# In the head slots of an attention kernel, turn the next pair's weights ahead of the last pair's attend

## The chip, the cores and the metric

One core of a Trainium2 chip. The metric is device time of one execution in microseconds (us), as the median of several runs. TensorE multiplies, VectorE (DVE), ScalarE (ACT) and GpSimd (POOL) work beside it, and SyncE (SP) issues the loads of the weights.

## What is computed

Two blocks in float32 on 256 tokens with 2048 channels. The first has two layers, each of a projection into seven parts, a gated depthwise convolution with LayerNorm, and a windowed attention with 16 heads of 64 and a sink logit; then an output projection, an embedding term and a gate. The second has one "fox" layer (32 heads, causal, with forget gates) and one sliding-window layer (32 heads, rotary positions, sink). The attention is where the change lies; in the first block it is

```python
s = jnp.einsum('bqkgd,bskd->bkgqs', qb, kb) * scale + bias_band
m = jnp.maximum(jnp.max(s, axis=-1), sink_f)
e = jnp.exp(s - m[..., None])
denom = jnp.sum(e, axis=-1) + jnp.exp(sink_f - m)
pr = (e / denom[..., None]).astype(vb.dtype)
return jnp.einsum('bkgqs,bskd->bqkgd', pr, vb)
```

and the causal ones do the same with a causal or a sliding mask. With 256 tokens there are two blocks of 128 queries and two of 128 keys.

## The kernel before

**Gemms.** Every projection is a chunk of 512 output columns and 2048 input channels. It is cut into 8 pieces of 256 channels. A piece is loaded by SP into one of four places of a ring (`stage`, L280 to L288), split by ScalarE into a rounded part `w_hi` (L1534) and by VectorE into the rest `w_lo` (L913), and used by TensorE with three terms (`w_hi` x high, `w_lo` x high, `w_hi` x low, L495 and L506). In the form "T" (weights stationary, L495) a piece is 24 products of 256 columns: two steps of 12. In the form "N" (L506) it is 12 products of 512 columns.

**Slots.** After each of the 16 steps of a chunk stands a slot, in which TensorE does other work (L512 to L515). The dictionary `work` says which: the functions in the list of slot n are called in their order, and so stand in TensorE's queue, which runs in order. Each of the other engines has a list of its own, written by hand as hooks behind its pieces (`chunk` at L915 and L1536).

**Attention.** Heads come in groups of 8, four pairs per group. One chunk of TensorE holds a group's scores (L596, into PSUM banks). VectorE adds the bias and finds the maxima (L1007), ScalarE takes the exponentials (L1543) into the tile `u`, VectorE divides by the sums in two lots of four heads (`norms`, L1024 to L1040, event `normed`). The next chunk has the group's `heads` (L651) in its slots, two steps apart from one another:

- `turn(kind, i)` (L612 to L624) transposes pair i's weights from `u` into the banks TB and SB, one head each: per head 4 transposes of 128x128 if all blocks count ("full", first block), 3 if causal. It waits for `t_free` (all copies so far are done, so the banks are free) and `normed`, and counts `pt_done` for each head.
- ScalarE copies each head's turned weights from its bank to the tile `pt` (`copy_turned`, L1593 to L1600), waits for `pt_done` and counts `t_free`.
- `attend(kind, i, values)` (L626 to L649) multiplies the values with pair i's turned weights in `pt` into the banks OB and MB, the two heads into the two halves of the output partitions. It waits for `t_free`, for i = 0 also for `s_free` and `ob_free`.

There is one `pt` for all pairs, so pair i+1 may be copied only once pair i has been attended. The group's five slots are: turn 0; attend 0, turn 1; attend 1, turn 2; attend 2, turn 3; attend 3. When `att_done` has come for all heads, VectorE multiplies by the gate (`gated`, L1042).

There are 12 such groups: 2 per layer of the first block (L765, L767, "full"), 4 in the fox layer (L825, in a loop of 3 and once more) and 4 in the sliding-window layer (L884, a loop of 3; the last, L887 to L889, in chunks of form "N"). `again(name, back)` (L97) gives a wait for the count that the event has reached so far in the engine's own order, less `back`.

`pt` also takes the 256 channels of `p` at the start of each layer of the first block (L1650), behind all attends.

Of the kernel before, what the change touches and what calls it, by code (L numbers as in the profile page):

```python
# [21 lines left out]
P = 128  # L22
# [3 lines left out]
NB = S // P  # L26
# [7 lines left out]
GH = CH // HD  # L34
# [37 lines left out]
              t_free=1, pt_done=1, weights_ready=1, ssq_done=2, ones_set=1)  # L72
# [72 lines left out]
def two_blocks(nc, x, p, norm_g, w_in, conv_w, conv_b, cln_g, cln_b, sink, rel_bias, w_out, w_pe, pe_g,  # L145
# [4 lines left out]
    with ExitStack() as ctx:  # L150
        def sb(name, shape, dt=F32):
            return ctx.enter_context(nc.sbuf_tensor(name, [P] + shape, dt))
# [19 lines left out]
        pt = sb("pt", [2, 4 * P])  # L172
# [23 lines left out]
        den = sb("den", [GH, NB])  # L196
        rden = sb("rden", [GH, NB])
        ck = sb("ck", [NB, 2, FH])

        rope = cacc[:, 0:2, :]  # L200
        rot = cacc[:, 2, 0:P]
# [17 lines left out]
        SB, TB, OB, MB = (AA[:, i * CH:(i + 1) * CH] for i in range(4))  # L219
# [239 lines left out]
        def half(j):  # L459
            return (j % 2) * HD  # L460
# [8 lines left out]
        def score_cols(kind, b):  # L469

            if kind == "full":
                return b * S, S
            return (0, P) if b == 0 else (P, S)
# [3 lines left out]
        def _(pe):  # L477
            t = Tally(sems, PER)
# [127 lines left out]
            def tiles(kind):  # L606

                return [(0, 0), (0, 1), (1, 0), (1, 1)] if kind == "full" else [(0, 0), (0, 1), (1, 1)]
# [3 lines left out]
            def turn(kind, i):  # L612

                def go():
                    pe.wait_ge(*t.again("t_free"))
                    pe.wait_ge(*t.see("normed", 2))
                    for j in (2 * i, 2 * i + 1):
                        for n, (kb, qb) in enumerate(tiles(kind)):
                            c, _ = score_cols(kind, qb)
                            mm = pe.transpose((TB, SB)[j % 2][:, n * P:(n + 1) * P], uw[:, j, c + kb * P:c + (kb + 1) * P],  # L620
                                              ident[:, :])
                        mm.then_inc(*t.inc("pt_done"))
                    t.skip("t_free", 2)
                return go  # L624

            def attend(kind, i, values):  # L626

                def go():
                    pe.wait_ge(*t.again("t_free"))
                    if i == 0:  # L630
                        pe.wait_ge(*t.again("s_free"))
                        pe.wait_ge(*t.again("ob_free"))
                    if i == 2:
                        pe.wait_ge(*t.again(misc_reader[0]))
                    dst, at = (OB, MB)[i // 2], (i % 2) * S
                    pairs = tiles(kind)
                    for kb in range(NB):
                        n = [x[0] for x in pairs].index(kb)
                        first = pairs[n][1]
                        for j in (2 * i, 2 * i + 1):  # L640
                            mm = pe.matmul(dst[half(j):half(j) + HD, at + first * P:at + S], values(j, kb),  # L641
                                           pt[:, j % 2, n * P:(n + NB - first) * P], start=i % 2 == 0 and kb == 0,
                                           stop=kb == NB - 1, skip_group_check=True)
                    mm.then_inc(*t.inc("att_done", 2))
                    if i == GH // 2 - 1:
                        t.skip("ob_free")
                        t.skip("mb_free")
                        misc_reader[0] = "mb_free"
                return go  # L649

            def heads(kind, values, at=0, extra=()):  # L651

                work = {}
                for i in range(GH // 2 + 1):
                    steps = []
                    if i > 0:
                        steps.extend(extra if i == 1 else ())
                        steps.append(attend(kind, i - 1, values))
                    if i < GH // 2:
                        steps.append(turn(kind, i))  # L660
                    work[at + 2 * i] = steps
                return work

# [42 lines left out]
            for l in range(depth):  # L706
# [56 lines left out]
                chunk("T", A, p1)  # L763
                chunk("T", A, p0, work=score_slots("full", keys1(0), (4, 10), keys_there))
                chunk("T", A, p1, work=heads("full", values1(0), 6))  # L765
                chunk("T", A, p0, work=score_slots("full", keys1(1), (3, 6, 9, 12), taken))
                chunk("T", A, p1, work=heads("full", values1(1), 6))  # L767
                chunk("T", A, p0)
                pe.wait_ge(*t.again("p_split"))
# [19 lines left out]
            for k in range(KT):  # L789
                if k == KT // 2:  # L790
                    spread_rs((diag, diag2))()
                for m, (w, xx) in enumerate(((w_hi, A[0]), (w_lo, A[0]), (w_hi, A[1]))):
                    mm = pe.matmul(OB[0:FH, 0:S], w[:, slot, k * FH:(k + 1) * FH], xx[:, k, :],  # L793
                                   start=k == 0 and m == 0, stop=k == KT - 1 and m == 2)
# [28 lines left out]
            def fox_attention():  # L823
                chunk("N", A, 0, work=score_slots("causal", fox_keys, (5, 10), taken))
                chunk("T", A, 1, work=heads("causal", fox_values, 7, [taken]))  # L825
# [692 lines left out]
        def _(act):  # L1518
            t = Tally(sems, PER)
# [25 lines left out]
            def high(dst, g, gain):  # L1545

                def go():
                    for k in range(4 * g, 4 * g + 4):
                        f_(dst[0][:, k, :], h[:, k, :], ACT.Copy, "x_rounded", scale=gain(k))
                return go  # L1550

            def square(g, src, first=True):

                def go():
                    act.wait_ge(*t.again("ssq_done", 1))
                    f_((gate, turned)[g % 2][:, :, :], src[:, 4 * g:4 * g + 4, :], ACT.Square, "sq_done")
                    t.skip("ssq_done")
                return go
# [12 lines left out]
            def gain_of(n):  # L1571

                return lambda k: both_gains[:, k:k + 1] if n == 4 else gains[:, n, k:k + 1]
# [19 lines left out]
            def copy_turned(kind, heads_):  # L1593

                n = (4 if kind == "full" else 3) * P
                def go():
                    for j in heads_:
                        act.wait_ge(*t.see("pt_done"))
                        act.copy(pt[:, j % 2, 0:n], (TB, SB)[j % 2][:, 0:n]).then_inc(*t.inc("t_free"))  # L1599
                return go  # L1600

            def gate_silu(chunks):
# [177 lines left out]
            for g in range(4):  # L1780
                def added():
                    act.wait_ge(*t.see("gemm_free"))
                steps = [added, high(A, g, gain_of(6)), square(g, h)]
# [162 lines left out]
```

## Time and profile before

| | |
|---|---|
| median of 3 runs | 1792.27 us |
| the three runs | 1784.59, 1792.27, 1794.22 us |
| the profiled execution | 1782.65 us |
| its span, first to last instruction | 1780.9 us |
| TensorE granted clock, mean | 0.998 of full |
| busy share of ScalarE | 51% |
| busy share of VectorE | 74% |
| mean rate from memory | 181 GB/s |

The rows quoted below come from the profiled execution. Times in them are from the start of its span. In rows of the time line the first number is the start, the second the duration in us of all that the row merges (x8: eight instructions), and each matmul row's end is modelled: a 256-column product is recorded at 0.28 us though the next one starts 0.11 us behind it.

### The profile page before, as it was taken

What the parts mean: (1) busy time and instruction counts of PE and PEld (TensorE: products, weight loads), DVE (VectorE), ACT (ScalarE), POOL (GpSimd) and SP (SyncE); (2) the same over time, 40 slices, a digit from 0 to 9 for tenths busy, and PEclk for the clock granted to TensorE, in tenths of its full rate; (3) what the DMA queues carried; (4) which work ended last, traced back from release to release, by engine and by line L of the source; (5) the groups of instructions that cost most, each with busy time, mean ns of one, the idle gap of its engine ahead of it and who ended that gap; (6) DMA issues with size and microseconds to landing.
All of it is one profiled execution on the core that took longest, in us unless ns stands there. A gap on an engine that the chain in (4) does not pass through costs nothing.

```text
span 1780.9 us, 35710 instructions
## 1 busy us (share of the span) xinstructions
PE 1762.0 (99%) x14365; PEld 1677.1 (94%) x14365; DVE 1311.4 (74%) x2088; ACT 900.0 (51%) x1326; POOL 40.1 (2%) x48
## 2 busy tenths in 40 slices
PE   8999999999999999999999999999999999999997
PEld 8999999999999999999999899998989999999876
DVE  7899899977679987998777765555565656666754
ACT  5433665545533456456565464545455443565553
POOL 0000000000000000000000110100100000000000
PEclk9999999999999999999999999999999999999999
DMA  7666655555666664556566666566655566545553
GB/s 232 189 207 190 190 143 175 191 190 194 196 186 207 192 200 142 155 191 199 180 201 185 203 184 202 181 201 182 195 165 165 191 190 174 155 146 162 161 190 130
DMA packets 199826, 325.54 MB, mean 183 GB/s; under 512 B 14783, under 2 KB 66191, under 8 KB 199565
## 3 DMA queue, kind: packets, MB, share of 16 engines
q1 hardware_dynamic: 197085, 320.85, 58.3%
q10 hardware_dynamic: 2608, 2.84, 0.5%
q8 instruction: 94, 1.54, 0.4%
q14 instruction: 39, 0.32, 0.1%
HBM read 320.42 MB, written 2.69 MB: 181 GB/s over the span
## 4 chain that ended last, share of the span: by engine, by line
PE 94%; DVE 5%; ACT 0%; issue 0%; DMA 0%; DVEq 0%; SPq 0%; ACTq 0%
PE g L495 73%; PE g L506 11%; PE att L641 2%; PE att L620 2%; PE att L596 2%; DVE w_lo L913 2%; DVE cacc L1159 2%; ACT w_hi L1534 0%; PE att L495 0%; PE att L793 0%; DMA stage<-in_w_in_dram 0%; PE att L850 0%; PE att L572 0%; PE att L873 0%; PE att L851 0%
## 5 line engine op out<-in xcount | busy, mean ns | idle before, releaser
L913 DVE TENSOR_TENSOR w_lo<-stage,w_hi 128x1024 fp32r<-128x1024 f32 x577 | 707.3, 1233 | 390.2 <-ACT w_hi L1534 389.3
L1534 ACT CAST w_hi<-stage 128x1024 fp32r<-128x1024 f32 x577 | 599.2, 1050 | 592.6 <-PE g L495 394.4
L495 PE MATMUL g<-a_hi,w_hi 128*128 128x256 f32 x2496 | 704.1, 282 | 2.5 <-DVE w_lo L913 1.6
L495 PE MATMUL g<-a_hi,w_lo 128*128 128x256 f32 x2496 | 693.6, 278 | 0.0
L495 PE MATMUL g<-a_lo,w_hi 128*128 128x256 f32 x2496 | 693.6, 278 | 0.0
L495 PEld LDWEIGHTS g<-a_hi,w_hi 128*128 128x128 f32 x2496 | 470.4, 188 | 12.8 <-issue 10.8
L495 PEld LDWEIGHTS g<-a_hi,w_lo 128*128 128x128 f32 x2496 | 470.3, 188 | 1.5 <-issue 1.2
L495 PEld LDWEIGHTS g<-a_lo,w_hi 128*128 128x128 f32 x2496 | 470.5, 188 | 0.0
L495 PE MATMUL g<-b_hi,w_hi 128*128 128x256 f32 x1440 | 403.1, 280 | 0.4 <-DVE w_lo L913 0.3
L495 PE MATMUL g<-b_hi,w_lo 128*128 128x256 f32 x1440 | 399.9, 278 | 0.0
L495 PE MATMUL g<-b_lo,w_hi 128*128 128x256 f32 x1440 | 399.9, 278 | 0.0
L495 PEld LDWEIGHTS g<-b_hi,w_hi 128*128 128x128 f32 x1440 | 270.8, 188 | 4.2 <-issue 2.9
L495 PEld LDWEIGHTS g<-b_hi,w_lo 128*128 128x128 f32 x1440 | 271.5, 189 | 0.1
L495 PEld LDWEIGHTS g<-b_lo,w_hi 128*128 128x128 f32 x1440 | 270.7, 188 | 0.0
L1159 DVE SCALAR_TENSOR_TENSOR cacc<-glu,cw,cacc 128x256 f32<-128x256 f32 x480 | 201.5, 476 | 0.2
L1543 ACT ACTIVATE u<-u,nbias 128x128 f32<-128x128 f32 (+1 forms) x192 | 88.1, 461 | 5.8 <-DVE nbias L1392 5.8
L1599 ACT COPY pt<-att 128x384 f32<-128x384 f32 (+1 forms) x96 | 44.6, 517 | 87.3 <-PE att L620 87.3
L506 PE MATMUL g<-w_hi,a_hi 128*128 128x512 f32 (+1 forms) x192 | 68.5, 357 | 0.0
L506 PE MATMUL g<-w_hi,a_lo 128*128 128x512 f32 (+1 forms) x192 | 68.2, 355 | 0.0
L506 PE MATMUL g<-w_lo,a_hi 128*128 128x512 f32 (+1 forms) x192 | 68.0, 354 | 0.0
L506 PE MATMUL g<-w_hi,b_hi 128*128 128x512 f32 (+1 forms) x156 | 57.9, 371 | 0.0
L506 PE MATMUL g<-w_lo,b_hi 128*128 128x512 f32 (+1 forms) x156 | 57.6, 370 | 0.0
(231 smaller groups left out, 1378.3 us busy)
## 6 DMA issues: line engine op xcount, KB each, us to landing
stage<-in_fox_w_in_dram SPq DMA_DIRECT2D x128, 512.0 KB, 4.1
stage<-in_w_in_dram SPq DMA_DIRECT2D x112, 512.0 KB, 3.9
stage<-in_swa_w_in_dram SPq DMA_DIRECT2D x72, 512.0 KB, 3.8
stage<-in_w_in_dram SPq DMA_DIRECT2D x128, 256.0 KB, 3.1
stage<-in_w_out_dram SPq DMA_DIRECT2D x64, 512.0 KB, 4.3
stage<-in_w_pg_dram SPq DMA_DIRECT2D x64, 512.0 KB, 4.1
stage<-in_fox_w_out_dram SPq DMA_DIRECT2D x32, 512.0 KB, 4.6
stage<-in_swa_w_out_dram SPq DMA_DIRECT2D x32, 512.0 KB, 4.3
```

Of the source, the lines that this page charges most:

```text
L495: mm = pe.matmul(acc[:, j * S:(j + 1) * S], w[:, slot, c0 + j * P:c0 + (j + 1) * P], xx[:, k, :], start=st and m == 0 and j % 2 == 0, stop ...
L506: mm = pe.matmul(acc[:, at:at + width], xx[:, k, b * P:(b + 1) * P], w[:, slot, col:col + width], start=st and m == 0 and (kind == "N" or ...
L596: mm = pe.matmul(score_bank(j, len(pairs))[:, c:c + n], q_of(j, b), keys(j)[:, 0:n], start=b == 0, stop=True, skip_group_check=True)
L620: mm = pe.transpose((TB, SB)[j % 2][:, n * P:(n + 1) * P], uw[:, j, c + kb * P:c + (kb + 1) * P], ident[:, :])
L641: mm = pe.matmul(dst[half(j):half(j) + HD, at + first * P:at + S], values(j, kb), pt[:, j % 2, n * P:(n + NB - first) * P], start=i % 2 == ...
L913: dve.tensor_tensor(w_lo[:, slot, :], stage[:, slot, :], w_hi[:, slot, :].bitcast(F32), ALU.subtract).then_inc(*t.inc("w_split"))
L1159: dve.scalar_tensor_tensor(out=cacc[:, c, :], in0=src, scalar=cw[:, c, l, k:k + 1], in1=cacc[:, c, :], op0=ALU.mult, op1=ALU.add).then_inc ...
L1534: act.copy(w_hi[:, slot, :], stage[:, slot, :]).then_inc(*t.inc("w_rounded"))
L1543: return act.activation(out, in_, func, **kw).then_inc(*t.inc(name))
L1599: act.copy(pt[:, j % 2, 0:n], (TB, SB)[j % 2][:, 0:n]).then_inc(*t.inc("t_free"))
```

## The change

In the three middle slots the order is turned round: the next pair's turn stands first, the last pair's attend behind it. The attend's wait for `t_free` is lowered by the two copies that the turn ahead of it has just announced, so that it still waits for its own pair alone; in the last slot, where no turn stands ahead, it is lowered by none. As pair i+1's turned weights may now be copied before or while pair i is attended, a second tile `pt2` is added, and pairs alternate between the two. The extra steps of the fox group's slot 1 (a wait for `gemm_free`, so that the values are there) still stand first in the slot.

```diff
@@ -196,6 +196,8 @@
         ck = sb("ck", [NB, 2, FH])
+        pt2 = sb("pt2", [2, 4 * P])
+        PT = (pt, pt2)
@@ -626,7 +628,7 @@ def attend(kind, i, values):
                 def go():
-                    pe.wait_ge(*t.again("t_free"))
+                    pe.wait_ge(*t.again("t_free", 2 if i < GH // 2 - 1 else 0))
                     if i == 0:
                         pe.wait_ge(*t.again("s_free"))
                         pe.wait_ge(*t.again("ob_free"))
@@ -639,7 +641,7 @@
                             mm = pe.matmul(dst[half(j):half(j) + HD, at + first * P:at + S], values(j, kb),
-                                           pt[:, j % 2, n * P:(n + NB - first) * P], start=i % 2 == 0 and kb == 0,
+                                           PT[i % 2][:, j % 2, n * P:(n + NB - first) * P], start=i % 2 == 0 and kb == 0,
@@ -653,11 +655,12 @@ def heads(kind, values, at=0, extra=()):
                 for i in range(GH // 2 + 1):
                     steps = []
-                    if i > 0:
-                        steps.extend(extra if i == 1 else ())
-                        steps.append(attend(kind, i - 1, values))
+                    if i == 1:
+                        steps.extend(extra)
                     if i < GH // 2:
                         steps.append(turn(kind, i))
+                    if i > 0:
+                        steps.append(attend(kind, i - 1, values))
                     work[at + 2 * i] = steps
@@ -1596,7 +1599,7 @@ def copy_turned(kind, heads_):
                         act.wait_ge(*t.see("pt_done"))
-                        act.copy(pt[:, j % 2, 0:n], (TB, SB)[j % 2][:, 0:n]).then_inc(*t.inc("t_free"))
+                        act.copy(PT[(j // 2) % 2][:, j % 2, 0:n], (TB, SB)[j % 2][:, 0:n]).then_inc(*t.inc("t_free"))
```

## Rows read from the trace of the kernel before

**Rows 1.** The page: TensorE's busy time, its weight loads', and the chain that ended last.

```profile
PE 1762.0 (99%) x14365; PEld 1677.1 (94%) x14365; DVE 1311.4 (74%) x2088; ACT 900.0 (51%) x1326; POOL 40.1 (2%) x48
...
PE 94%; DVE 5%; ACT 0%; issue 0%; DMA 0%; DVEq 0%; SPq 0%; ACTq 0%
```

**Rows 2.** Waits of TensorE: who waited for whom, total us, times, longest.

```profile
PE g L495 <- DVE w_lo L913: 2.3, 5, 0.8
```

**Rows 3.** Waits of ScalarE, the row of the copies.

```profile
ACT pt L1599 <- PE att L620: 87.3, 40, 2.8
```

**Rows 4.** Time line of TensorE, first full group: slots 0, 1 and 4.

```profile
189.23 0.28 PE L495 MATMUL g<-a_lo,w_hi 128*128 128x256 f32 x1
189.34 1.04 PE L620 MATMUL att<-ident,u 128*128 128x128 f32 x8
190.14 0.36 PE L495 MATMUL g<-a_hi,w_hi 128*128 128x256 f32 x1
...
192.93 0.28 PE L495 MATMUL g<-a_lo,w_hi 128*128 128x256 f32 x1
193.14 1.08 PE L641 MATMUL att<-pt,v 128*64 128x256 f32 x8
194.16 1.09 PE L620 MATMUL att<-ident,u 128*128 128x128 f32 x8
...
195.21 0.28 PE L495 MATMUL g<-a_hi,w_lo 128*128 128x256 f32 x1
...
207.74 1.08 PE L641 MATMUL att<-pt,v 128*64 128x256 f32 x8
...
208.98 0.28 PE L495 MATMUL g<-a_hi,w_lo 128*128 128x256 f32 x1
```

**Rows 5.** Time line of TensorE, first fox group: slots 0, 1 and 4.

```profile
1033.79 0.28 PE L495 MATMUL g<-a_lo,w_hi 128*128 128x256 f32 x1
1033.91 0.82 PE L620 MATMUL att<-ident,u 128*128 128x128 f32 x6
...
1037.19 0.28 PE L495 MATMUL g<-a_lo,w_hi 128*128 128x256 f32 x1
...
1039.03 0.28 PE L495 MATMUL g<-a_hi,w_lo 128*128 128x256 f32 x1
...
1050.60 0.87 PE L641 MATMUL att<-pt,v 128*64 128x256 f32 x8
...
1051.62 0.28 PE L495 MATMUL g<-a_hi,w_lo 128*128 128x256 f32 x1
```

**Rows 6.** Time line of ScalarE: the copies of pair 0 and pair 1, first group.

```profile
190.59 1.06 ACT L1599 COPY pt<-att 128x512 f32<-128x512 f32 x2
...
194.85 1.08 ACT L1599 COPY pt<-att 128x512 f32<-128x512 f32 x2 [2.25 <-PE att L620]
```

**Rows 7.** Time line of VectorE: the second lot of norms, first group.

```profile
191.36 2.50 DVE L1038 TENSOR_TENSOR u<-u,rden 128x512 f32<-128x512 f32 x4
```

**Rows 8.** TensorE by stretches: us, busy (products), granted clock, DMA share, GB/s.

```profile
195.40:197.70 2.30, 2.30 (x22) 1.00 0.66 158
...
337.00:372.00 35.00, 35.00 (x300) 1.00 0.62 202
390.00:440.00 50.00, 50.00 (x444) 1.00 0.60 194
...
1039.20:1041.50 2.30, 2.30 (x22) 1.00 0.80 241
1043.60:1045.90 2.30, 2.30 (x23) 1.00 0.98 313
...
1054.00:1064.00 10.00, 10.00 (x91) 1.00 0.37 108
```

## The prediction

> **What bounds the kernel now.** I read the page first. TensorE's matmul row is busy for 99% of the span, the weight-load row for 94%, and the chain that ended last is 94% TensorE; the span has only 1780.9 - 1762.0 = 18.9 us in which no matmul was under way [rows 1]. Second I read the waits. The longest wait of a TensorE product on another engine sums to 2.3 us (five products waiting for `w_lo`), and no row says that an attend (L641) or a turn (L620) waited for anyone [rows 2]. ScalarE does wait for the turns, 87.3 us in 40 places [rows 3], but it is busy for half the span, and its idle time costs nothing while TensorE doesn't wait for it. So a gain can come only from how TensorE's own instructions follow each other in the 36 slots that change.
>
> **Which slots.** There are 12 groups of heads: 4 full (two per layer of the first block) and 8 causal (4 fox, 4 sliding window). Each has five slots: a turn alone, three slots with both, an attend alone. Only the three in the middle change order: 12 full and 24 causal slots. Their contents stay the same, and so do all loads and stores.
>
> **What is removed: a wait.** In a middle slot both orders wait first for the same thing, all copies of the last pair: the turn needs its banks back, the attend its weights. Pair 0's copies end at 190.59 + 1.06 = 191.65, and the last gemm product before slot 1 starts at 192.93 [rows 4, 6]: 1.3 us of room. The wait costs nothing now, so the new order can't buy it back. The attend's wait, two back, asks for the same count as the turn's before it. No queue of SP or POOL is passed, and no DMA is moved; the last slot is unchanged, so SP's wait for `att_done` and VectorE's gating come at the same point.
>
> **What comes earlier: the turn, by one attend** (194.16 - 193.14 = 1.02 us [rows 4], about 0.8 in causal groups). It now needs its normalised weights that much sooner. Pair 1's are in the first lot of norms, with pair 0's, for which slot 0 has waited already. The second lot is done at 191.36 + 2.50 = 193.86 [rows 7]; its first use is slot 2's turn, one stretch of gemm products behind slot 1, at 195.21 + 22 x 0.118 = 197.8 [rows 4, 8]. No new wait, with 3.9 us of room. ScalarE's copies start earlier too, 12 x 1.02 + 24 x 0.8 = 31 us in all. That empties the wait of [rows 3] to some 56 us, and the time reappears as waiting for the ring of rounded weights or for loads. TensorE sees none of it. If this cover were gone, each late copy would cost a slot what it is late by.
>
> **What is exchanged on TensorE.** I measure a slot from the start of the last gemm product before it to the start of the second one behind it, because the first one behind it has a longer spacing of its own.
> - Full, attend then turn: 195.21 - 192.93 = 2.28 us [rows 4].
> - Full, turn then attend: the last of eight transposes starts at 189.34 + 1.04 - 0.27 = 190.11 (a transpose is recorded at 0.27), that is 0.88 after the gemm product at 189.23. Then comes the seam from a turn to an attend, which the trace doesn't have. Behind it, attend to second gemm product: 208.98 - 207.74 = 1.24.
> - The seam, from both sides. Nearest row: gemm product to attend, 193.14 - 192.93 = 0.21, where two gemm products stand 0.11 apart. Low end: as a turn gives way to a gemm product, 190.14 - 190.11 = 0.03. High end: as an attend gives way to a turn, 194.16 less the attend's last start (193.14 + 1.08 - 0.38 = 193.84) = 0.32. I take 0.21, since it leads into the same instruction from the same full-width shape.
> - So 0.88 + 0.21 + 1.24 = 2.33, 0.05 more than now; low end 2.15 (-0.13), high end 2.44 (+0.16).
> - Causal, now: 1039.03 - 1037.19 = 1.84. New: last transpose at 1033.91 + 0.82 - 0.27 = 1034.46, 0.67 after the gemm product; + 0.21; + 1051.62 - 1050.60 = 1.02; together 1.90, so +0.06; ends -0.12 and +0.17 [rows 5].
> - Sum: 12 x 0.05 + 24 x 0.06 = +2.0 us; ends -4.4 and +6.0.
>
> The drain at these seams is in the rows: 0.10 more than the usual spacing before every attend, the same whether the copy had ended long before or not. The page "TensorEngine Tiling (Array Packing)" of the Trainium skill, section Key Properties, says that a change of tiling mode drains TensorE. The attend is 128x64, all round it is 128x128, so by that rule a slot has one change in and one out in both orders, the turn shielding neither: it speaks against any gain in the order itself, which is what the nearest rows give too. By the rule and by the row the sum stays at about +2; it would be -4.4 only if the turn hid the way in.
>
> **What the gemm products between the slots do.** The trace shows two spacings of the same 256-column product at the same granted clock of 1.00. Counting a product as in a window if its 0.28 us overlap it: 300 in 35.00 us make 35.28 / 300 = 0.1176 us, 444 in 50.00 make 0.1132 [rows 8]. So there is a slow and a fast spacing, 4.3 ns apart, and each lasts until something interrupts the stream. Behind a turn in a middle full slot it is the slow one (22 in 2.30 us), and in causal groups it is slow behind slots 1 and 3 (22) and fast behind slot 2 (23). Behind the last slot, where the attend stands last, it is the fast one (91 in 10.00 us) [rows 8]. In the new order every middle slot ends with an attend. If that settles the spacing, 12 full and 2 x 7 causal stretches of some 22 spacings get faster: 26 x 22 x 0.0043 = -2.5 us (the eighth causal group runs beside 512-column products, for which I see no such pair). At worst the fast stretches behind slot 2 turn slow: +0.7.
>
> **Sum:** +2.0 - 2.5 = -0.5 us; ends -6.9 and +6.7. Against the profiled execution, 1782.65 us, that is 1782.2. The three timed runs are higher (1784.59, 1792.27, 1794.22): the same program scatters over 11.6 us, more than all I sum. The median less 0.5 is 1791.8; since the middle of the four executions is 1788.4, I give 1790. What this kernel's measurement can tell from no change is about 0.5%, 9 us.
>
> **The second buffer** adds 4 KB per partition behind all other tiles, so no address moves. ScalarE writes the same sizes. Zero; nothing hides it, as there is no instruction more.
>
> **Rivals.**
> 1. *The turn hides the way into the attend, and the spacing gets fast.* All low ends: -6.9 us, 1785 against the median. For: the transposes need TensorE for only 0.11 each. Against: the gap before an attend is there behind dense gemm products too. Chance 0.08, and it would still mostly read as "same".
> 2. *Slower: the stream leaves each group in the slow spacing.* Place: the gemm products behind a group's last slot, which run in the fast one now [rows 8]. Behind the fox groups lie ten chunks of 192 products, behind the others about four more: 14 x 192 x 0.0043 = 11.6 us, so 1804. It decides as soon as the spacing depends on more than the last instruction group before the stream, for instance on where in the two-product rhythm it resumes. Against: the last slot is untouched, and its attend follows gemm products as before. Chance 0.08.
> 3. *Faster: long slow stretches turn fast.* The 35 us stretch shown would give 35 x 0.0043 / 0.1176 = 1.3 us; it takes some 250 us of such stretches for 9 us, so 1783 or less needs a change far from the edit. Chance 0.08.
> 4. *The edit relieves a wait that the records hide.* If the 0.10 before an attend were the wait for the copies and not a drain, 36 x 0.10 = -3.6 us with the seam gone: 1788. Against: it is 0.21 in [rows 4] with a copy ended 1.3 us before. Chance 0.04, read as "same".
>
> The forecast has the remaining 0.72.
>
> **How the numbers follow.** Over 0.5% faster: rival 3 and a quarter of rival 1, 0.10. Slower: rival 2, 0.08. Within 0.5%: 0.82. The range takes the four known executions with part of the ends: 1782.65 less 3, and 1794.22 plus 5. It holds the forecast with its scatter and rivals 1, 3 in part and 4, and leaves out rival 2.
>
> **What the changed profile would show.** Right: TensorE busy 99%, no wait on L641 or L620; a full middle slot at 2.33 +- 0.05 and a causal one at 1.90; 23 instead of 22 products in 2.30 us between slots; ScalarE's wait for turns near 56 us. Wrong: a turn or attend listed as waiting, a slot of 2.15 (the seam is hidden), or 420 products behind a fox group at 0.1176.

## The result, and the profile after

| | before | after |
|---|---|---|
| median of 15 runs each | 1788.14 us | 1799.04 us |
| lowest to highest | 1782.90 to 1794.22 us | 1792.33 to 1802.83 us |
| the profiled execution | 1782.65 us | 1802.28 us |
| its span | 1780.9 us | 1800.5 us |

The change makes the kernel slower: 1.0056 times the time before, 95% interval 1.0041 to 1.0071, or 10.9 us between the medians. The forecast was 1790.0 with a range to 1799.0 and no change as the likeliest case; the median lies 0.04 us outside the range, and the case that came true had a chance of 0.08.

Line numbers move by two or three: the gemm products are L497, the turns L622, the attends L643, the copies L1602. First the page of the kernel after: span, busy time by engine, and the engines' shares of the chain that ended last.

```profile
span 1800.5 us, 35709 instructions
...
PE 1779.9 (99%) x14365; PEld 1693.4 (94%) x14365; DVE 1311.7 (73%) x2088; ACT 900.4 (50%) x1326; POOL 41.4 (2%) x48
...
PE 90%; DVE 8%; SPq 1%; ACT 1%; issue 1%; DMA 0%; DVEq 0%; ACTq 0%
```

Against [rows 1] the number of products is the same, 14365, and TensorE is busy for 1779.9 - 1762.0 = 17.9 us more, of 19.6 us that the span has grown. The other 1.7 us are waits: TensorE waited 9.1 us in all before and 10.8 after. VectorE has 8% of the chain where it had 5%, but TensorE's waits for it are only 1.0 us longer (3.0 before, 4.0 after). The same products take longer. The waits of TensorE (who waited for whom, total us, times, longest), after and then, beside [rows 2], before:

```profile
PE att L685 <- DMA cacc<-in_norm_g_dram: 6.8, 1, 6.8
PE g L497 <- DVE w_lo L916: 2.6, 6, 0.8
PE g L497 <- DVE a_lo L1096: 1.4, 2, 1.2
```

```profile
PE att L682 <- DMA cacc<-in_norm_g_dram: 5.8, 1, 5.8
PE g L495 <- DVE a_lo L1093: 0.7, 1, 0.7
```

No turn (L622) and no attend (L643) is in the list, as was forecast; the rows named `att` are other products that write the same banks. The wait for `w_lo` is 0.3 us above [rows 2]. ScalarE's waits, the three longest:

```profile
ACT w_hi L1537 <- PE g L497: 428.3, 249, 3.9
ACT w_hi L1537 <- PE g L508: 84.9, 44, 3.4
ACT pt L1602 <- PE att L622: 76.8, 40, 2.9
```

The wait for turns fell by 10.5 us from [rows 3]. TensorE sees nothing of it.

**The slots.** The time line of TensorE after, the first full group's slot 1 and the first fox group's slots 1 and 4:

```profile
194.15 0.28 PE L497 MATMUL g<-a_lo,w_hi 128*128 128x256 f32 x1
194.27 1.03 PE L622 MATMUL att<-ident,u 128*128 128x128 f32 x8
195.23 1.08 PE L643 MATMUL att<-pt,v 128*64 128x256 f32 x8
196.25 0.39 PE L497 MATMUL g<-a_hi,w_hi 128*128 128x256 f32 x1
196.47 0.28 PE L497 MATMUL g<-a_hi,w_lo 128*128 128x256 f32 x1
...
1047.33 0.28 PE L497 MATMUL g<-a_lo,w_hi 128*128 128x256 f32 x1
1047.45 0.82 PE L622 MATMUL att<-ident,u 128*128 128x128 f32 x6
1048.20 0.87 PE L643 MATMUL att<-pt,v 128*64 128x256 f32 x8
1049.00 0.39 PE L497 MATMUL g<-a_hi,w_hi 128*128 128x256 f32 x1
1049.22 0.28 PE L497 MATMUL g<-a_hi,w_lo 128*128 128x256 f32 x1
...
1060.72 0.87 PE L643 MATMUL att<-pt,v 128*64 128x256 f32 x8
```

From the last gemm product before a slot to the second behind it: full 196.47 - 194.15 = 2.32 us, causal 1049.22 - 1047.33 = 1.89. The forecasts were 2.33 and 1.90.

**The gemm products between.** TensorE by stretches of equal length, after: us, busy (products), granted clock, DMA share, GB/s.

```profile
390.00:440.00 50.00, 50.00 (x427) 1.00 0.57 183
855.00:905.00 50.00, 50.00 (x427) 1.00 0.52 170
1065.00:1090.00 25.00, 25.00 (x214) 1.00 0.62 188
1165.00:1190.00 25.00, 25.00 (x215) 1.00 0.59 187
1370.00:1420.00 50.00, 50.00 (x427) 1.00 0.56 176
```

The same stretches before (390:440, with 444, is in [rows 8]):

```profile
855.00:905.00 50.00, 50.00 (x443) 1.00 0.59 189
1065.00:1090.00 25.00, 25.00 (x223) 1.00 0.74 226
1165.00:1190.00 25.00, 25.00 (x223) 1.00 0.76 232
1370.00:1420.00 50.00, 50.00 (x444) 1.00 0.56 180
```

Here is the time. Counted as the prediction counts, 50.28 / 444 = 0.1132 us per product before and 50.28 / 427 = 0.1178 after, at a granted clock of 1.00 in all of them. The slow spacing of the prediction stands in stretches that were in the fast one before. By the starts of single products the two are 0.1133 and 0.1178, 4.4 ns apart.

Which stretches: the three last rows lie behind fox groups. In all, 384 + 384 + 384 + 774 = 1926 products without an interruption stand there: 1926 x 4.4 ns = 8.5 us. How the delay grows there can be read from the last attend of the first and the fourth fox group: it starts at 1050.60 [rows 5] and 1343.08 before, at 1060.72 and 1359.22 after, so 10.1 us late and then 16.1 us.

```profile
1343.08 0.87 PE L641 MATMUL att<-pt,v 128*64 128x256 f32 x8
```

```profile
1359.22 0.87 PE L643 MATMUL att<-pt,v 128*64 128x256 f32 x8
```

The first two rows of the two tables lie in the output part of the first block's two layers, 1068 and 1020 products in one piece, 4.7 and 4.5 us. In before's profile both are fast and in after's both slow; further down one program shows both spacings in the second of them.

### The profile page after: what moved, and what is told of

Same layout as the page of the kernel before. It is cut to its first block, busy times and chain, and to the rows that moved or that the text cites. A ratio compares the mean times of both kernels' runs of the same rounds, so it can differ in the third digit from the quotient of the medians.

```text
span 1800.5 us, 35709 instructions
## 1 busy us (share of the span) xinstructions
PE 1779.9 (99%) x14365; PEld 1693.4 (94%) x14365; DVE 1311.7 (73%) x2088; ACT 900.4 (50%) x1326; POOL 41.4 (2%) x48
## 4 chain that ended last, share of the span: by engine, by line
PE 90%; DVE 8%; SPq 1%; ACT 1%; issue 1%; DMA 0%; DVEq 0%; ACTq 0%
PE g L497 71%; PE g L508 11%; DVE w_lo L916 3%; DVE cacc L1162 3%; PE att L643 2%; PE att L598 2%; PE att L622 2%; ACT w_hi L1537 0%; SPq L310 0%; PE att L796 0%; DMA stage<-in_w_in_dram 0%; SPq L288 0%; DVE glu L1134 0%; PE att L876 0%; PE att L854 0%
## 5 line engine op out<-in xcount | busy, mean ns | idle before, releaser
L497 PE MATMUL g<-a_hi,w_hi 128*128 128x256 f32 x2496 | 707.9, 284 | 3.4 <-DVE w_lo L916 1.9
L497 PE MATMUL g<-a_lo,w_hi 128*128 128x256 f32 x2496 | 696.6, 279 | 0.0
L497 PE MATMUL g<-a_hi,w_lo 128*128 128x256 f32 x2496 | 696.4, 279 | 0.0
L497 PEld LDWEIGHTS g<-a_hi,w_hi 128*128 128x128 f32 x2496 | 473.2, 190 | 20.1 <-issue 17.1
L497 PEld LDWEIGHTS g<-a_hi,w_lo 128*128 128x128 f32 x2496 | 468.7, 188 | 1.5 <-issue 1.2
L497 PEld LDWEIGHTS g<-a_lo,w_hi 128*128 128x128 f32 x2496 | 469.8, 188 | 0.0
L497 PE MATMUL g<-b_hi,w_hi 128*128 128x256 f32 x1440 | 406.1, 282 | 0.1
L497 PE MATMUL g<-b_hi,w_lo 128*128 128x256 f32 x1440 | 402.7, 280 | 0.0
L497 PE MATMUL g<-b_lo,w_hi 128*128 128x256 f32 x1440 | 402.7, 280 | 0.0
L497 PEld LDWEIGHTS g<-b_hi,w_hi 128*128 128x128 f32 x1440 | 273.8, 190 | 6.2 <-issue 5.2
L497 PEld LDWEIGHTS g<-b_hi,w_lo 128*128 128x128 f32 x1440 | 270.9, 188 | 0.1
L497 PEld LDWEIGHTS g<-b_lo,w_hi 128*128 128x128 f32 x1440 | 270.6, 188 | 0.0
L1602 ACT COPY pt<-att 128x384 f32<-128x384 f32 (+1 forms) x96 | 44.6, 516 | 76.8 <-PE att L622 76.8
L508 PE MATMUL g<-w_hi,b_lo 128*128 128x512 f32 (+1 forms) x156 | 57.7, 370 | 0.0
```

The source lines that it names most:

```text
L497: mm = pe.matmul(acc[:, j * S:(j + 1) * S], w[:, slot, c0 + j * P:c0 + (j + 1) * P], xx[:, k, :], start=st and m == 0 and j % 2 == 0, stop ...
L508: mm = pe.matmul(acc[:, at:at + width], xx[:, k, b * P:(b + 1) * P], w[:, slot, col:col + width], start=st and m == 0 and (kind == "N" or ...
L1602: act.copy(PT[(j // 2) % 2][:, j % 2, 0:n], (TB, SB)[j % 2][:, 0:n]).then_inc(*t.inc("t_free"))
```

## Experiments

The kernels ran in five sets, each on one chip together with the kernel before. Before itself had a median of 1784.41, 1786.52, 1787.06, 1792.13 and 1788.00 us in the five sets, so medians are compared within a set only, and the counts of products in the profiled execution are the sharper instrument. "Behind fox" is the stretch 1165:1190, in which a fast spacing shows 223 products and a slow one 214 or 215; 390:440 and 855:905 show 444 or 443 fast, 427 or 426 slow. All kernels compute everything that the reference does. In some, transposes are added whose result nobody reads.

### First set: which part of the change (before 1784.41 us)

**buffer_only**: two tiles for turned weights, the old order.

```diff
+        pt2 = sb("pt2", [2, 4 * P])
+        PT = (pt, pt2)
-                                           pt[:, j % 2, n * P:(n + NB - first) * P], ...
+                                           PT[i % 2][:, j % 2, n * P:(n + NB - first) * P], ...
-                        act.copy(pt[:, j % 2, 0:n], ...
+                        act.copy(PT[(j // 2) % 2][:, j % 2, 0:n], ...
```

> Two buffers as in the change, but attend before turn in every slot, as before. The theory of the two spacings (what ends a group sets whether the gemm products behind it come at 0.1133 or 0.1176 us, and the new order leaves the fox groups in the slow one): as the kernel before, ratio 1.000, and 384 products behind a fox group at 0.113. Rival, the second buffer itself (reads of pt2 by the last attend set the slow spacing or cost time): ratio 1.005, slow behind the fox groups.

Measured: 1793.44 us, ratio 1.0049 [1.0035, 1.0063]. Stretches of its TensorE:

```profile
390.00:440.00 50.00, 50.00 (x443) 1.00 0.58 194
855.00:905.00 50.00, 50.00 (x444) 1.00 0.56 188
...
1165.00:1190.00 25.00, 25.00 (x215) 1.00 0.67 216
1370.00:1420.00 50.00, 50.00 (x427) 1.00 0.54 187
```

Not one instruction more than before, in the order of before, and the loss is there: 0.49% of 1784.41 is 8.7 us, where 1926 slow products give 8.5. The long stretches of the first block are fast in this execution and in before's, so their spans can be compared too: 1790.6 - 1780.9 = 9.7 us, where the streams behind the fox and the sliding-window groups give 8.5 + 0.8.

**causal_only** and **full_only**: both tiles, the new order in one kind of group.

```diff
+            def ahead(kind, slot):
+                return kind == "causal" and 0 < slot < GH // 2      # full_only: kind == "full"
```

> New order in the eight causal groups only. Two spacings: the three stretches of 384 and the one of 774 products behind the fox groups are slow, 1926 x 4.4 ns = 8.5 us, so a ratio near 1.005, with two bands of the same program's scatter on top. Rival, the direct cost of the seams (0.06 us in each of 24 slots): 1.4 us, ratio 1.001.

> New order in the four full groups only. Two spacings: the stretch behind a full group is fast in both orders, so ratio 1.000 (within 1 us), unless the two long stretches of 1068 and 1020 products in the output part of each layer, slow in the changed kernel's profile, are set slow by this (then +9 us, ratio 1.005). Rival, direct cost of the seams: 12 x 0.05 = 0.6 us.

Measured: causal_only 1794.10 us, 1.0054 [1.004, 1.0067]; full_only 1793.55 us, 1.0053 [1.0039, 1.0067]. Both have 214 or 215 products behind fox. In full_only the fox groups are in the old order, so it is again the tile. The order itself adds nothing that these intervals can tell from the seams' +1.2 us (24 causal slots at 0.05) and +0.5 us (12 full ones at 0.04).

**all_pad1**: the whole change, and one transpose of the unit matrix behind the last attend of each causal group.

```diff
                     mm.then_inc(*t.inc("att_done", 2))
+                    if i == GH // 2 - 1 and kind == "causal":
+                        pe.transpose(TB[:, 0:P], ident[:, :], ident[:, :])
```

> The change, and behind the last attend of every causal group one transpose more (of the unit matrix, into the free bank TB, read by nobody). Two spacings as a matter of how the stream is interrupted: the extra instruction can flip the stretch behind it back to fast, then 8.5 us less than the change, ratio 1.001 to before, though it adds 8 x 0.11 = 0.9 us of work. Rival, the order itself costs (work late on another engine): ratio 1.006, a little over the change's.

Measured: 1783.65 us, 0.9996 [0.9986, 1.0005]. Its time line behind the first fox group, then its stretches:

```profile
1051.57 0.87 PE L646 MATMUL att<-pt,v 128*64 128x256 f32 x8
1052.37 0.33 PE L652 MATMUL att<-ident 128*128 128x128 f32 x1
1052.46 0.37 PE L497 MATMUL g<-a_hi,w_hi 128*128 128x256 f32 x1
```

```profile
1165.00:1190.00 25.00, 25.00 (x223) 1.00 0.68 216
1370.00:1420.00 50.00, 50.00 (x443) 1.00 0.54 183
```

One transpose, 1052.46 - 1052.37 = 0.09 us, and the stream behind it is fast. The loss is gone, although both the second tile and the new order are still there. The long stretches are fast in this execution too, and its span is 1781.9 us, 1.0 above before's. So what the change costs apart from the stream behind the groups is about 1 us. Its loss comes from leaving that stream in the slow one of two states.

### Second set: is it the alignment of the tile? (before 1786.52 us)

`pt2` starts at byte 216788 of a partition, which is no multiple of 64; `pt`, at 164800, is.

```diff
+        sb("spacer", [11])                   # buffer_aligned, change_aligned: ahead of pt2
+        pt2 = sb("pt2", [2, 4 * P])
```
```diff
+        sb("shift", [5])                     # before_shifted: before, with pt 20 bytes further on
         pt = sb("pt", [2, 4 * P])
+        sb("shift2", [11])
```

**before_pad1** is the kernel before with all_pad1's transpose.

> As buffer_only, but pt2 starts at a multiple of 64 bytes, as pt does; before it lay 20 bytes behind a multiple of 32. Theory of the place (products that read a tile lying across 64-byte lines end the slot a few ns elsewhere, and that flips the spacing of the stream behind): as before, 8.5 us less than buffer_only, ratio 1.000, 384 products behind a fox group at 0.113. Rival, any second buffer does it: ratio 1.005.

> The change, with pt2 at a multiple of 64 bytes. Theory of the place: the new order alone costs only its seams, about 2 us, less what the spacing between the slots gives back, so ratio 1.000 to 1.001, and the stretches behind the fox groups are fast. Rival, order and place each flip the spacing: the new order too leaves the fox groups slow, ratio 1.005.

> The kernel before with one thing different: pt starts 20 bytes behind a multiple of 64 (all later tiles keep their alignment). Theory of the place: the flips in the head slots change and 384 products behind a fox group may be slow, up to 8.5 us more (with all four attends shifted, not two, an even number of flips could cancel: then the slots differ, but the stretch is fast). Rival, place is nothing: every stretch as before.

> The kernel before, with one transpose more behind the last attend of each causal group. If one instruction more flips the spacing whatever it was, the 1926 products behind the fox groups go slow: +8.5 us and 0.9 us of work, ratio 1.005. Rival, a transpose of 128 full columns there always leaves the fast spacing: ratio 1.0005.

| | median us | ratio | behind fox |
|---|---|---|---|
| buffer_aligned | 1796.04 | 1.0046 [1.0031, 1.006] | 215, slow |
| change_aligned | 1797.08 | 1.0049 [1.0032, 1.0067] | 214, slow |
| before_shifted | 1790.90 | 1.0019 [1.0003, 1.0036] | 223, fast |
| before_pad1 | 1788.59 | 1.0000 [0.9986, 1.0015] | 223, fast |

That `pt2` isn't aligned to 64 bytes is not the cause: an aligned second tile loses the same, and the first one moved off its alignment keeps the fast stream behind fox. (The 20 bytes do change something: before_shifted has the slow spacing behind all middle slots of its causal groups, and the fast one behind 10 of its 12 middle full slots, where before has the slow one. Both of its long stretches are slow in the profile.) before_pad1 tells what the transpose does. If it changed over whatever spacing the attend leaves, the stream behind before's attends, which is fast, would now be slow. It stays fast, and in all_pad1, where the attend alone leaves the slow one, it becomes fast.

### Third set: does the distance matter? (before 1787.06 us)

```diff
+        pt2 = sb("pt2", [2, 4 * P])          # buffer_near, change_near: directly behind pt
         turned = sb("turned", ...
```
```diff
-        pt = sb("pt", [2, 4 * P])            # pt_at_end: one tile, behind all others,
+        sb("gap", [2 * 4 * P])               # and nothing else moved
         ...
+        pt = sb("pt", [2, 4 * P])
```

**pads** is the kernel before with one transpose at the end of every short interruption that the attention doesn't make (the statistics, L560; their spreading, L572; the sum and the spreading of LayerNorm), 17 in all, meant to make the first block's long stretches fast.

> Old order and two buffers, the second directly behind the first (4 KB on, all later tiles 4 KB further). Theory of the place: near the first, slot 2 flips the spacing as in the kernel before and the stretch behind a fox group is fast, ratio 1.000. Rival, alternating between two tiles is what does it, wherever they lie: 384 products behind a fox group at 0.118, ratio 1.005.

> The change with the second buffer directly behind the first. If the place alone was the fault: the new order costs its seams alone, ratio 1.000 to 1.002. If the new order has a part of its own in the flips: slow behind the fox groups all the same, ratio 1.005.

> The kernel before with its one buffer moved to where the change put the second (an unused tile keeps all others in place). Theory of the place: slots 1 to 3 all in the slow spacing behind the turn, since every attend reads from the far place; behind the last slot the attend flips it to fast, as with the shifted tile, so ratio 1.000 to 1.001. Rival, alternation: every slot as before (slow, fast, slow).

> The kernel before, with one transpose of the unit matrix (result read by nobody) as the last instruction of each statistic, spread and LayerNorm product outside the attention. A transpose behind an attend left the fast spacing whatever came in; if it does so behind these too, the stretches of 336, 324, 372 and the smaller ones, some 1740 products now slow, come at 0.1133 (-7.7 us), the two of 1068 and 1020 are always fast (they are slow in some executions), and 14 transposes cost 1.6 us: 6 to 12 us faster, ratio 0.993 to 0.997. Rival, the transpose settles nothing there: ratio 1.001.

| | median us | ratio | 390:440 | 855:905 | behind fox |
|---|---|---|---|---|---|
| buffer_near | 1792.29 | 1.0021 [1.0005, 1.0038] | 427 | 427 | 223 |
| change_near | 1790.65 | 1.0022 [1.0005, 1.0038] | 444 | 427 | 223, behind the first 214 |
| pt_at_end | 1790.08 | 1.0014 [1.0004, 1.0024] | 427 | 444 | 223 |
| pads | 1782.06 | 0.9979 [0.9965, 0.9993] | 443 | 444 | 223 |

The second tile directly behind the first doesn't slow the stream behind fox, the same tile 52 KB on does. (In buffer_near and change_near all tiles behind the first one lie 4 KB further on as well, in before_shifted 64 bytes. In buffer_only and pt_at_end nothing has moved but what the text names.) To see why, read the spacing between the slots. In the time line the distance from one attend to the next holds 24 gemm products and a turn, and is 0.1 us longer when the spacing is slow. First fox group, kernel before (its last attend, 1050.60, is in [rows 5]), then buffer_only, then pt_at_end:

```profile
1037.39 0.87 PE L641 MATMUL att<-pt,v 128*64 128x256 f32 x8
...
1041.83 0.87 PE L641 MATMUL att<-pt,v 128*64 128x256 f32 x8
...
1046.16 0.87 PE L641 MATMUL att<-pt,v 128*64 128x256 f32 x8
```

```profile
1037.64 0.87 PE L646 MATMUL att<-pt,v 128*64 128x256 f32 x8
...
1042.08 0.87 PE L646 MATMUL att<-pt,v 128*64 128x256 f32 x8
...
1046.51 0.87 PE L646 MATMUL att<-pt,v 128*64 128x256 f32 x8
...
1050.85 0.87 PE L646 MATMUL att<-pt,v 128*64 128x256 f32 x8
```

```profile
1043.54 0.87 PE L642 MATMUL att<-pt,v 128*64 128x256 f32 x8
...
1047.97 0.87 PE L642 MATMUL att<-pt,v 128*64 128x256 f32 x8
...
1052.40 0.87 PE L642 MATMUL att<-pt,v 128*64 128x256 f32 x8
...
1056.84 0.87 PE L642 MATMUL att<-pt,v 128*64 128x256 f32 x8
```

Before: 4.44, 4.33, 4.44, that is slow, fast, slow, and the stream behind is fast. buffer_only: 4.44, 4.43, 4.34, slow, slow, fast, and behind it slow. pt_at_end: 4.43, 4.43, 4.44, all slow, and behind it fast. Two rules give all three, for causal groups in the old order. **An attend that stands alone changes the spacing to the other one.** And **an attend with a turn behind it changes it over too if it reads the tile in its old place, but leaves the slow one behind, whatever was before, if it reads the tile at the far place.** (Full groups are different: in all 19 profiles the lone attend at their end leaves the fast spacing, and in the kernel before every middle slot leaves the slow one.) The changing over at the old place, or 4 KB from it, holds in all 105 middle slots of the causal groups of five kernels (before, buffer_near, before_pad1, pads, old_order_pads); the slow one was left in 41 of 42 with the one tile moved (pt_at_end and pt_mid, below), and in all 28 second slots of the four kernels with a far second tile in the old order. The first and third slots of those four read the old place and change over, 56 of 56. With the one tile 20 bytes on (before_shifted) the slow one was left in all 21 too, so it isn't distance alone. buffer_only differs from before in the second slot's attend alone, which reads `pt2`: it leaves slow where there was a change to fast, the third slot changes slow to fast, and the last attend turns the stream slow.

The first rule holds in every causal group, the last group left out, of the 13 kernels (before and after among them) that have no transpose behind the last attend: 91 of 91 groups change over, 44 from fast to slow and 47 from slow to fast. Where one transpose follows it, six kernels, all 42 groups go on fast, 17 of them from fast.

change_near fits the first rule: in its first fox group the spacing is fast before the last attend and slow behind it, in the others slow and then fast. So the tile's place is not all of it: with the near tile the new order still leaves one fox stream of four slow, and one of the three behind sliding-window groups, 444 x 4.4 ns = 2.0 us. With 1.7 us for the seams that is 3.7, where 1.0022 is 3.9. Why the new order with the near tile stays fast throughout the first group and not in the others isn't settled.

pads makes stretches fast that are slow in the kernel before. The part of the first layer behind 510 us, before and then pads:

```profile
515.00:545.00 30.00, 30.00 (x257) 1.00 0.55 165
```

```profile
515.00:545.00 30.00, 30.00 (x267) 1.00 0.57 176
```

The longest that become fast are 324 + 324 + 372 = 1020 products, 4.5 us, and most of the 336 products that start at 49 us, about 1 us. The 17 transposes cost 17 x 0.09 = 1.5. Measured are 3.7 us [1.3, 6.3], less than the 6 to 12 that were expected.

Outside the attention the transpose is not a sure means. Behind these 17 interruptions the first products are in the slow spacing in 217 of 255 cases in the 15 kernels without the transposes. In the four kernels with them (pads and three below) it is 5 of 68. One of the five is the stretch of 1020 products in change_pads.

### Fourth and fifth set: both orders with transposes added (before 1792.13 and 1788.00 us)

**change_pads** is the whole change with the near `pt2`, the transpose behind the last attend of causal groups, and pads; **change_pads_b** the same kernel once more, beside **old_order_pads**, which differs from it in the order of turn and attend alone (`ahead` returns `False`). **pt_mid** has the one tile between its old place and the end, 41920 bytes (42 KB) on; the tiles behind it lie 4 KB further on than before. **far_pad1** is buffer_only with all_pad1's transpose.

> The change with its second buffer directly behind the first, one transpose behind the last attend of each causal group, and one behind each statistic, spread and LayerNorm product. If the flips explain the whole loss, this holds every long stretch in the fast spacing and is as fast as pads, ratio 0.997 to 0.999, its seams costing 2 us at most. Rival, the new order has a cost of its own beyond them: ratio over 1.002.

> The kernel before with its one buffer 41 KB further on (between cm and ident, 10 KB short of the far place). If distance within the memory decides: the far pattern already here (slots slow, slow, slow) or still the near one (slow, fast, slow), and this tells between which places it changes; the stretch behind a fox group is fast either way, ratio 1.000 to 1.002.

> buffer_only (old order, second buffer far off) with one transpose behind the last attend of each causal group. If the loss of buffer_only is the slow spacing behind the fox groups and nothing else, it is gone: ratio 1.000 to 1.001, 384 products there at 0.113. Rival, alternation costs in another way: ratio 1.004 still.

> As change_pads in everything (second buffer near, every transpose added), but the attend first in each slot, as before. If the order is worth only its seams and the stretches between the slots, this differs from change_pads by under 3 us. Rival, the new order gains by itself once the flips are settled: 5 us or more slower than change_pads, ratio over 0.997.

> change_pads once more, on the same chip as old_order_pads, so that the two can be compared: ratio 0.993 to 0.997.

| | median us | ratio | 390:440 | 855:905 | behind fox |
|---|---|---|---|---|---|
| change_pads | 1781.93 | 0.9944 [0.9929, 0.9958] | 443 | 427 | 223 |
| pt_mid | 1792.55 | 1.0003 [0.9989, 1.0016] | 427 | 444 | 223 |
| far_pad1 | 1792.00 | 0.9999 [0.9987, 1.001] | 427 | 426 | 223 |
| old_order_pads | 1782.85 | 0.9973 [0.9957, 0.9989] | 444 | 443 | 223 |
| change_pads_b | 1782.64 | 0.9974 [0.9962, 0.9987] | 444 | 444 | 223 |

far_pad1 takes buffer_only's loss away (1.0049 to 0.9999) with the far tile still in use, so apart from the state that it leaves the far tile costs nothing that the interval [0.9987, 1.001] shows. pt_mid has the slots of pt_at_end, slow behind the middle ones, so the far behaviour is there at 42 KB already; it is level with the kernel before of its set. With the transposes added the two orders are equal, 1782.64 and 1782.85 us. Both are about 5 us under the kernel before of their set. The change's own idea is worth nothing that these medians show, and as the two orders are level, the gain is that of the transposes. The one kernel run twice has 0.9944 and 0.9974 against two befores of 1792.13 and 1788.00 and nearly the same median: the scatter is before's more than its own.

**The scatter.** change_pads was profiled in an execution of 1786.04 us with 427 products in 855:905, change_pads_b, the same program, in one of 1782.09 us with 444:

```profile
855.00:905.00 50.00, 50.00 (x427) 1.00 0.54 184
```

```profile
855.00:905.00 50.00, 50.00 (x444) 1.00 0.57 190
```

The spans, 1784.2 and 1780.3 us, differ by 3.9, where 1020 slow products give 4.5 and shorter stretches give some of it back. So one program takes one spacing or the other in a long stretch from execution to execution. Two such stretches of 4.7 and 4.5 us would give times some 4.6 us apart in three heaps, and before's 15 runs can be read so (three from 1782.90 to 1784.59, seven from 1786.24 to 1789.74, five from 1791.37 to 1794.22). The 15 runs after can be read in the same way (three from 1792.33 to 1794.05, five from 1796.95 to 1799.04, seven from 1801.32 to 1802.83), and the mean of each heap is 9.5 to 10.0 us above its like before. It is a reading, as only one execution of each kernel was profiled.

## Why the prediction was wrong

- **The number**: a change of -0.5 us was forecast and +10.9 was measured. That the median misses the range by only 0.04 us is no near hit: the range reached so high because it allowed 5 us above the slowest run of the kernel before.
- **What bounds the kernel**: right. TensorE is busy for 99% both times, no turn or attend waits, and 17.9 of the 19.6 us between the spans are time in which the same products are under way. The longest wait of all was not the 2.3 us that the prediction read, though, but 5.8 us for a load (L682), which the edit doesn't touch.
- **What is removed, what comes earlier**: right that the removed wait was worth nothing and that the second lot of norms is ready in time. ScalarE's wait was forecast at 56 us and is 76.8: the copies do start earlier, but the wait moves with them more than it shrinks. Nothing hung on it.
- **The seams**: right. The seam from the last transpose to the attend was taken at 0.21 between 0.03 and 0.32. After, the last transpose starts at 194.27 + 1.03 - 0.27 = 195.03 and the attend at 195.23: 0.20. By the rule of the Trainium skill that the prediction cited ("TensorEngine Tiling (Array Packing)", Key Properties: a change of tiling mode drains TensorE) the turn can't shield the attend, and the trace agrees. Slots of 2.32 and 1.89 where 2.33 and 1.90 were forecast, so 12 x 0.04 + 24 x 0.05 = 1.7 us where 2.0 were forecast.
- **The gemm products between the slots, -2.5 us**: wrong. It was hung on "if that settles the spacing", that is, on the last instruction group deciding it. Behind attends in the new order the profile has both spacings: fast in all three slots of the first fox group, but slow, slow, fast in the three others, slow in most of the full ones. Counted over the profile, 26 of the 33 stretches behind middle slots (the last group's left out, as in the prediction) are slow before and 21 after: 5 x 22 x 4.4 ns = 0.5 us.
- **The second buffer, "Zero; nothing hides it, as there is no instruction more"**: this is the step that failed, and the one that decided. The argument was about instructions and about the old tiles' addresses. But the attends of pairs 1 and 3 now read from another place, and buffer_only shows that this alone costs 8.7 us [6.2, 11.2]: a different state, left in one slot and handed on through the rest, comes out at a group's end as the slow spacing of up to 774 products.
- **Rival 2** named the place, the price and the condition: the stream behind the groups goes slow, 11.6 us, "as soon as the spacing depends on more than the last instruction group before the stream". That came true, and so did the sign that was to show it, some 420 products behind a fox group in the slow spacing: 384 and up to 774. Behind fox 8.5 us, behind the three sliding-window groups 180 products or 0.8 us; with the seams 11.0, less 0.5 between the slots, and the medians differ by 10.9. So close a fit owes something to luck, as the median of either kernel also depends on how many of its runs had a long stretch slow. What spoke against it, "the last slot is untouched, and its attend follows gemm products as before", missed that what those gemm products hand over is not the same: their spacing. The rows already had a hint. Spacings of slow, fast, slow behind three slots of the same contents (the first two are in [rows 8]) can't come from the last instruction group alone, and a chance of 0.08 was too small for the only rival that took this up.
- **The price of rival 2**: ten chunks behind fox were right (1926 products); "about four more" behind the others were too many. The last attend of a full group leaves the stream fast in all 76 full groups of the 19 profiles, so only the sliding-window groups' short stretches were lost.
- **The scatter**: taken as given, 11.6 us in three runs. In the centre 1790 it was right enough for before, but it was probably a sign of the same mechanism (the heaps above), and the profiled execution (1782.65) was one with both long stretches fast.

## What to carry to other kernels

Where a dense stream of equal matmuls shows two spacings at the same clock, treat the spacing as a state that each interruption hands on, and price every edit in a slot, a tile's new place included, by the longest stream behind it: count the products in equal windows behind each interruption, before and after. If some cheap instruction at the end of the interruption leaves the fast state (here a transpose, 0.09 us, behind an attend 42 times in 42, elsewhere 63 in 68), it takes most of the dependence on what stands before out of the time; count again to see where it did. An edit that is measured without that may be credited or blamed for the state alone.

## What the runs showed of the hardware that was not expected

- 256-column products stand 113.3 or 117.8 ns apart at a granted clock of 1.00, and keep to one of them for up to 1068 products on end. In this kernel that is worth 16 us between the two profiled executions: some 3800 slow spacings before and 7500 after, 3700 x 4.4 ns.
- What changes it is an interruption. In causal groups an attend alone changes it over, 91 times in 91. One transpose of the unit matrix behind it leaves it fast, 42 times in 42. Behind interruptions outside the attention the same transpose left it fast 63 times in 68, so it is no certain rule.
- The place of the tile that the interrupting products read is part of it: in causal groups 4 KB further on behaves as the old place, 42 and 52 KB further on otherwise, and so does one 20 bytes further on. So neither distance nor a multiple of 64 bytes explains it alone, and which property of the place does isn't settled. Places between 4 and 42 KB were not tried.
- In a long stretch of the first block (1020 products) the same program took either spacing in two executions, and the heaps of run times suggest the same of the other (1068). Why is open, and whether the place of a tile changes how often: buffer_near has the slots of the kernel before in every group, and is still at 1.0021 [1.0005, 1.0038], with both long stretches slow in its profile.
